# Turning the rotary halves: a float32 product on TensorE against a lane shuffle on VectorE

## The reference, cut to what matters

```python
def apply_partial_rope(x, cos, sin):
    half = ROPE_DIM // 2                      # ROPE_DIM = 16 of the 64 features of a head
    xr = x[..., :ROPE_DIM].astype(jnp.float32)
    x1, x2 = xr[..., :half], xr[..., half:]
    rot = jnp.concatenate([x1 * c - x2 * s, x2 * c + x1 * s], axis=-1)
    return jnp.concatenate([rot.astype(x.dtype), x[..., ROPE_DIM:]], axis=-1)

u = rmsnorm(x, norm_mix[l])
proj = u @ w_in[l]                            # q, k, v, iq, ik, iw, cB, cC, ch, g
q, k, iq, ik = (apply_partial_rope(...) for each)
y_attn = dsa_attention(q, k, v, iq, ik, iw) @ w_attn_out[l]
```

## Time and profile before

| | us |
|---|---|
| median of three runs | 1742.22 (1742.13 to 1742.66) |
| the profiled execution, device time | 1742.58 |
| its span in the trace | 1741.2 |
| TensorE busy with products | 1719.8 |
| VectorE busy | 1330.1 |
| ScalarE busy | 917.9 |

### The profile page before, as it was taken

How to read it: one execution, slowest core, us unless ns; L and a number is a source line. 1 busy time by engine, 2 the same in 40 slices (tenths; PEclk the granted TensorE clock), 3 DMA queues, 4 the chain that set the end, 5 groups by cost and what they waited for, 6 DMA issues and landing times.

```text
span 1741.2 us, 33420 instructions
## 1 busy us (share of the span) xinstructions
PE 1719.8 (99%) x11698; PEld 1582.1 (91%) x11698; DVE 1330.1 (76%) x2375; ACT 917.9 (53%) x1624; POOL 63.8 (4%) x113
## 2 busy tenths in 40 slices
PE   9999999999999999999999999999999999999997
PEld 8899899989999899999889999999999988888886
DVE  6986788778976788877765999988888766666666
ACT  4354544444454544455554555577777655555553
POOL 0000001000000122100000000000000000000000
PEclk9999999999999999999999999999999999999999
DMA  6556688754544699744344555554443456555654
GB/s 229 170 177 205 212 293 276 245 182 158 169 158 159 228 326 323 240 153 134 121 170 136 172 175 181 181 171 137 142 134 134 138 193 193 193 192 192 193 193 153
DMA packets 90250, 327.76 MB, mean 188 GB/s; under 512 B 11016, under 2 KB 11192, under 8 KB 89712
## 3 DMA queue, kind: packets, MB, share of 16 engines
q1 hardware_dynamic: 79056, 286.45, 49.6%
q0 software_dynamic: 9840, 34.82, 6.2%
q10 hardware_dynamic: 1264, 5.24, 0.8%
HBM read 324.34 MB, written 6.09 MB: 190 GB/s over the span
## 4 chain that ended last, share of the span: by engine, by line
PE 82%; DVE 13%; issue 2%; ACT 1%; DMA 1%; DVEq 0%; ACTq 0%; SPq 0%
PE bank L209 25%; PE bank L210 24%; PE bank L211 24%; DVE Z L86 6%; DVE w_lo L186 4%; PE bank L1767 3%; DVE yc L86 1%; PE bank L280 1%; PE bank L1325 1%; PE bank L480 1%; ACT w_hi L181 1%; DVE rows L86 0%; PE bank L773 0%; PE bank L1594 0%; PE bank L1181 0%
## 5 line engine op out<-in xcount | busy, mean ns | idle before, releaser
L186 DVE TENSOR_TENSOR w_lo<-raw,w_hi 128x1024 fp32r<-128x1024 f32 x544 | 658.8, 1221 | 157.1 <-ACT w_hi L181 156.0
L181 ACT ACTIVATE w_hi<-raw 128x1024 fp32r<-128x1024 f32 x544 | 572.3, 1054 | 260.6 <-PE bank L211 203.3
L209 PE MATMUL bank<-u_hi,w_hi 128*128 128x256 f32 x2400 | 692.9, 289 | 2.8 <-DVE Z L86 1.3
L210 PE MATMUL bank<-u_lo,w_hi 128*128 128x256 f32 x2400 | 678.7, 283 | 0.0
L211 PE MATMUL bank<-u_hi,w_lo 128*128 128x256 f32 x2400 | 678.6, 283 | 0.0
L209 PEld LDWEIGHTS bank<-u_hi,w_hi 128*128 128x128 f32 x2400 | 459.5, 191 | 15.5 <-issue 7.9
L210 PEld LDWEIGHTS bank<-u_lo,w_hi 128*128 128x128 f32 x2400 | 459.9, 192 | 4.4 <-issue 2.2
L211 PEld LDWEIGHTS bank<-u_hi,w_lo 128*128 128x128 f32 x2400 | 459.5, 191 | 0.0
L209 PE MATMUL bank<-w_hi,a_hi 128*128 128x512 f32 x744 | 290.3, 390 | 0.7 <-DVE u_lo L1853 0.7
L210 PE MATMUL bank<-w_lo,a_hi 128*128 128x512 f32 x744 | 290.1, 390 | 0.0
L211 PE MATMUL bank<-w_hi,a_lo 128*128 128x512 f32 x744 | 289.4, 389 | 0.0
(11 more groups left out here) (283 smaller groups left out, 1715.6 us busy)
## 6 DMA issues: line engine op xcount, KB each, us to landing
raw<-stream SPq DMA_DIRECT2D x544, 512.0 KB, 4.2
gate<-w_ada POOLq DMA_DIRECT2D x48, 512.0 KB, 6.0
t_rows<-t_by_distance POOLq DMA_DIRECT2D x8, 256.0 KB, 3.7
rpb_rows<-rpb_pad POOLq DMA_DIRECT2D x8, 224.0 KB, 4.2
bias_b<-rpb_rows POOLq DMA_DIRECT2D x16, 96.0 KB, 6.5
bias_a<-t_rows POOLq DMA_DIRECT2D x1, 1536.0 KB, 12.6
x<-x_in ACTq DMA_DIRECT2D x2, 512.0 KB, 5.7
gains_b<-gains POOLq DMA_DIRECT2D x1, 1024.0 KB, 9.3
```

The lines of the kernel that those rows point to most:

```text
L181: nc.scalar.activation(w_hi[:, s, :], raw[:, s, :], ACT.Copy).then_inc(s_hi, 1)
L186: nc.vector.tensor_tensor(w_lo[:, s, :], raw[:, s, :], w_hi[:, s, :].bitcast(F32), ALU.subtract).then_inc(s_split, 1)
L209: M.matmul(o, lh, rh, start=start, stop=False, skip_group_check=True)
L210: M.matmul(o, lh, rl, start=False, stop=False, skip_group_check=True)
```

## The change

The permutation is no longer a product. `rope` calls VectorE's `stream_shuffle`, which reorders partitions within each group of 32 by one list, `SWAP` (the first 8 lanes trade places with the next 8; where a group holds no rotary features the sine is 0, so that the order there does not matter). The sine product then reads the shuffled copy `rot` in SBUF instead of a bank. `ik` is turned on 64 partitions, and a second shuffle with the identity list copies it to the other 64.

`R` is no longer multiplied in when `k` and `ik` leave their banks: ScalarE copies them out as they are, and two new tables `RC` and `RS` (cosine and sine times `R`) made by VectorE right after `R` take its place. The table in DRAM is smaller (cosine and sine once each, no permutation matrices) and comes by one DMA instead of two.

```diff
+SWAP = [(p + ROPE // 2) % ROPE if p < ROPE else p for p in range(32)]
@@ main_part
                     if name == "ik":
-                        got["iwT"] = AC.go((m,), S.activation, ikT[DH:DH + 32, :], bank[b][DH:DH + 32, 0:T], ACT.Copy)
-                        ik_m = m
-                    elif name == "k":
-                        if f == 0:
-                            ik_m = VE.go((ik_m, got["R"], got["iwT"]), V.tensor_tensor, ikT[0:DH, :], bank[4][0:DH, 0:T],
-                                         R[0:DH, :], ALU.mult)
-                            got["ik", 0], free[4] = ik_m, (ik_m,)
-                        m = VE.go((m, got["R"]), V.tensor_tensor, d.rearrange("p (a n) -> p a n", a=parts),
-                                  bank[b][:, 0:parts * T].rearrange("p (a n) -> p a n", a=parts),
-                                  R.unsqueeze(1).to_broadcast([P, parts, T]), ALU.mult)
+                        m = AC.go((m,), S.activation, ikT[0:DH + 32, :], bank[b][0:DH + 32, 0:T], ACT.Copy)
                     else:
-                        m = AC.go((m,), S.activation, d, bank[b][:, 0:parts * T], ACT.Copy)
+                        m = AC.go((m,), S.activation, dst[:, f:f + 2, :].rearrange("p a n -> p (a n)"), bank[b][:, :],
+                                  ACT.Copy)
@@ the turn
-                t = PE.done(M.matmul(bank[b][:, 0:n], turn[:, 0:P], d, start=True, stop=True))
-                m = VE.go((t, got.get(("rot", b))), V.tensor_tensor, r, bank[b][:, 0:n],
-                          rope[:, 1, 0:n], ALU.mult)
-                m1 = VE.go((t, got[name, f]), V.tensor_tensor, d, d, rope[:, 0, 0:n], ALU.mult)
+                m = VE.go((got[name], got.get(("rot", slot))), V.stream_shuffle, r, d, SWAP)
+                m1 = VE.go((m,), V.tensor_tensor, d, d, cos, ALU.mult)
+                m = VE.go((m,), V.tensor_tensor, r, r, sin, ALU.mult)
                 m = VE.go((m, m1), V.tensor_tensor, d, d, r, ALU.add)
@@ rope_of_ik
-                for j in range(2):
-                    i = M.matmul(bank[b][:, j * T:(j + 1) * T], turn[0:DH, (1 + j) * P:(2 + j) * P], ikT[0:DH, :],
-                                 start=True, stop=True, skip_group_check=True)
+                m = rope(ikT[0:DH, :], rot[0:DH, 0, 0:T], (0, ("ik", 0)), RC[0:DH, :], RS[0:DH, :])
+                got["ik", 0, "r"] = VE.go((m, got["iw"]), V.stream_shuffle, ikT[DH:2 * DH, :], ikT[0:DH, :],
+                                          list(range(32)))
@@ side_part
                 m = VE.go((t,), V.tensor_copy, R, bank[6][:, 0:T])
+                VE.go((m,), V.tensor_tensor, RC, R, rope_t[:, 0, :], ALU.mult)
+                VE.go((m,), V.tensor_tensor, RS, R, rope_t[:, 1, :], ALU.mult)
                 got["R"] = VE.go((m,), V.tensor_tensor, R2, R, R, ALU.mult)
```

More of the change, by code:

```diff
@@ L516, in build @@
         ph1a = ph1.enter_context(ExitStack())
-        rope = sb(ph1a, "rope", [P, 2, 2 * T])
-        turn = sb(ph1a, "turn", [P, 3 * P])
+        rope_t = sb(ph1a, "rope", [P, 2, T])
+        rc_rs = sb(ph1a, "rc_rs", [P, 4, T])
+        RC, RS = rc_rs[:, 0, :], rc_rs[:, 1, :]
         cw_all = sb(ph1a, "cw_all", [P, LAYERS, KW * TAPS])
@@ L783, in rope_of_ik, with rope @@
-            def rope_of_ik():
[L785 to L788, removed]
-                for j in range(2):
-                    i = M.matmul(bank[b][:, j * T:(j + 1) * T], turn[0:DH, (1 + j) * P:(2 + j) * P], ikT[0:DH, :],
-                                 start=True, stop=True, skip_group_check=True)
[L792 to L799, removed]
+            def rope(d, r, names, cos, sin):
+                slot, name = names
+                VE.wait((s_rope, 16), got.get("R"))
+                m = VE.go((got[name], got.get(("rot", slot))), V.stream_shuffle, r, d, SWAP)
+                m1 = VE.go((m,), V.tensor_tensor, d, d, cos, ALU.mult)
+                m = VE.go((m,), V.tensor_tensor, r, r, sin, ALU.mult)
+                m = VE.go((m, m1), V.tensor_tensor, d, d, r, ALU.add)
+                got["rot", slot] = m
+                got[(*name, "r")] = m
+                return m
@@ new lines, in rope_of @@
+            def rope_of(name, dst, f, slot):
+                cos, sin = (a.unsqueeze(1).to_broadcast([P, 2, T]) for a in (
+                    (RC, RS) if name == "k" else (rope_t[:, 0, 0:T], rope_t[:, 1, 0:T])))
+                rope(dst[:, f:f + 2, :], rot[:, slot, :].rearrange("p (a n) -> p a n", a=2), (slot, (name, f)), cos, sin)
+            def rope_of_ik():
+                m = rope(ikT[0:DH, :], rot[0:DH, 0, 0:T], (0, ("ik", 0)), RC[0:DH, :], RS[0:DH, :])
+                got["ik", 0, "r"] = VE.go((m, got["iw"]), V.stream_shuffle, ikT[DH:2 * DH, :], ikT[0:DH, :],
+                                          list(range(32)))
@@ L820, in side_part @@
                 m = VE.go((t,), V.tensor_copy, R, bank[6][:, 0:T])
+                VE.wait((s_rope, 16))
+                VE.go((m,), V.tensor_tensor, RC, R, rope_t[:, 0, :], ALU.mult)
+                VE.go((m,), V.tensor_tensor, RS, R, rope_t[:, 1, :], ALU.mult)
                 got["R"] = VE.go((m,), V.tensor_tensor, R2, R, R, ALU.mult)
@@ L824, in side_part @@
                 take(6)
-                PE.wait(got["iwT"])
+                PE.wait(got["ik", 0])
                 for tt in range(NT):
@@ L1999, in rope_table @@
     cos, sin = np.ones((P, T), np.float32), np.zeros((P, T), np.float32)
-    turn = np.zeros((P, P), np.float32)
     for f in range(P):
@@ L2005, in rope_table @@
             sin[f] = np.sin(ang[:, d % half]) * (-1.0 if d < half else 1.0)
[L2006 to L2010, removed]
+    return np.concatenate([cos, sin], 1)
 def t5_table_of_distance():
```

29 lines of the change are left out of this document (8 added, 21 removed).

## The result

The changed kernel takes **1750.43 us** (median of 6 runs, 1749.53 to 1752.22) against 1742.45 for the kernel before on the same chip (6 runs, 1742.13 to 1742.88). The ratio is 1.0047, with a 95% interval of 1.0035 to 1.0059: slower by 8.0 us. The profiled execution was the slowest of the six, at 1752.22 us with a span of 1750.9, so it shows 9.7 us of span more than the one before, where the median shows 8.0.

What follows compares the result with a forecast made beforehand. Both engines were taken as full in this stage, with VectorE's turns deciding when attention starts: 1742.58 + 2.9 + 2.2 (lateness per layer) + 3.0 (slow clock) = 1750.7, stated as 1750.3 us against the median; range 1743.5 to 1755.

Steps and rivals of the forecast that it cites:

- Where the end is set: At the first attention product (line 425 before, 426 after): net VectorE work beyond its 0.6 and 0.3 us lead delays it.
- The large turn: One 512-column turn on VectorE: 1.99 us before, 2.85 after, so 0.86 more, shuffle priced as a tensor_tensor plus 0.08 load.
- The cheap shuffle: Rival: a large turn costs 0.35 us less, giving 1743, with up to 3 more for the clock; chance 14%.
- the dear one: Rival: the shuffle takes twice the time per element, 6.4 us more, 1756.7; chance 7%.
- Ahead of the first index scores: VectorE work up to the index scores: +0.04 us in the first layer, 0.9 earlier in the second.
- From there to line 426: Four turns add 3.44 us to VectorE; the first attention product comes 2.9 and 2.2 us later in the two layers.
- The stands: TensorE waits some 6 us per layer ahead of the attention scores, and 2 and 1 us for ikT.
- The slow clock: Lower TensorE clock after each 6 us stand: 1.5 us each, 3.0 in all, with ends of 0 and 6.
- The nearest rival, late without a slow clock: VectorE is late as forecast but TensorE's resting costs nothing: 1747.3 us; chance 24%.

Runs made afterwards that it cites:

- e5: Changed kernel with the attention issued two pieces later and two side-part steps taken out further on, so both parts end together; 1735.16 us.
- e3: Changed kernel with each shuffle of k and q made twice; 1757.03 us.
- e6: Changed kernel with k and q turned by float32 products on TensorE again, iq and ik keeping the shuffle; 1740.53 us.
- e9: Balanced kernel (attention two pieces later, two steps out) with index scores one piece later too and one step of second-tile exponentials taken out; 1738.51 us.
- e1: Changed kernel with 24 unneeded products of 512 columns put on TensorE ahead of the attention scores; 1746.18 us.
- e10: Balanced kernel (attention two pieces later, two steps out) with 7 unneeded products where TensorE stands for ikT in the first layer; 1734.89 us.
- e4: Changed kernel with the attention issued two pieces later, by two empty side-part steps ahead of it; 1742.27 us.
- e2: Changed kernel without the shuffles of k and q, which are then not rotated as the reference does; 1745.68 us.

## Why the prediction was right

The forecast was 1750.3 us and the time is 1750.4. The mechanism held; that the sum fits to 0.1 us is luck, since its terms do not.

- **Where the end is set.** Right. TensorE's spared products are real (e5 has 9.6 us less busy time with the dip in it, where I counted 10.3), and none of it reached the end, since line 426 waits for VectorE. The row that carried this was the earlier trace rows, one wait of 0.2 us in 46, against the 76% of the earlier trace rows. e3 doubles the shuffles and pays for each in full, e6 takes them away and the loss goes.
- **The large turn.** 2.71 us against 2.85. The tensor_tensor as the nearest row was the right choice: the shuffle takes 0.72 to 0.74 us, 0.77 from start to start. My error is the load of the lane list, which I priced at 0.08 after the earlier trace rows and which costs nothing. The cheap shuffle and the dear one both fall. What the Trainium skill, "VectorE: DVE Perf Modes", perf-mode tier table, says of the shuffle (one element per cycle only) agrees with this 0.74: with the 0.43 of the shuffle of 256 columns that is 1.2 ns per further column, and 2400 ns for 2048 is 1.2 too. The 0.6 that I had scaled from it was short by 0.14.
- **Ahead of the first index scores.** I said +0.04 for the first layer, and the scores start 0.60 earlier. Of that 0.43 is the earlier beginning of the execution, so that -0.17 stands against the +0.04: the turn of `iq` is 0.14 less than priced and that of `ik` 0.19 (2.21 for 2.40), and waits between the other rows give back 0.12. In the second layer I said -0.9 and it is -1.2 (417.95 - 5.05 - 414.12).
- **From there to line 426.** Four turns add 4 x 0.72 = 2.9, not 3.44. The leads were also smaller than I took them: from the end of the last addition to line 426 the signal takes 0.26 us (84.54 to 84.80, and 464.94 to 465.20), and I had taken off under 0.1, so VectorE was ready 0.40 and 0.10 early, not 0.6 and 0.3. By this account 2.9 - 0.17 - 0.40 = 2.3 and 2.9 - 1.2 - 0.1 = 1.6 us would be VectorE's own; by place it holds TensorE up by 2.00 and 1.55, where I said 2.9 and 2.2. This term was too large by 1.5; the 0.3 in the first layer I did not trace. The 3.04 measured there looks like my 2.9 only because the clock's dip after the shorter stand adds 1.47.
- **The stands.** About 6 us predicted in each layer, 5.80 and 6.38 measured. For `ikT` 2 and 1 predicted, 1.84 and 0.55 measured.
- **The slow clock.** The mechanism is right and its size was off, the other way: 3.0 predicted, 6.3 in the profiled execution, and 8.0 - 3.55 = 4.4 in the median. The start of the program was the wrong measure for a stand in the middle: here the clock stays at half for some 4 and 6 us after the work resumes, and 2.0 and 2.8 us are lost, not 1.5 each. The row itself also varies, from 6.00 us (after) to 7.63 (e9), and the clock column does not show that start: in the trace of after it reads 1.00 from 2 to 4 us with 6 products recorded, and from 4 to 6 us with 11. And I let only the two long stands count, while one of 1.84 us can do it. The rule that I cited from the Trainium skill, "TensorE: Matmul & The Clock Gate", on HAM oscillation (a long enough gap lowers the clock), is thus shown in mid-program by these rows and by e1, with the reservation that for stands of about 2 us length alone does not decide, as the last section says.

So the mechanism, the place and the size of the stands held, and the time came out to 0.1 us because two terms were off by like amounts in opposite directions, 1.5 too much for VectorE and 1.4 too little for the clock. The nearest rival, late without a slow clock at 1747.3, is struck by the rows at 0.50 and by e1.

I had also taken the order of the side part as given. The changed kernel does not gain, as I said, but a gain was there to be had in another order, 7.1 us under the kernel before (5.3 under the same order without shuffles), behind two empty steps ahead of line 426 and two steps less behind it.

## What to carry to other kernels

Work moved to an engine that is idle on the average is paid in full if, in the stage where it lands, that engine never waits and another waits for it: read its waits in that stage and the lead at the next place where the two meet, not its share. If the lead is too short, issue the consumer later and shorten the woven part elsewhere by as many steps, since two more steps alone only moved the stand to the end of the stage. And count a stand of TensorE with the slow clock behind it, 2.0 and 2.8 us here, which needless products in its place take away.

## What was not expected

- A stand of TensorE of 1.8 to 1.9 us, with full work before it, is followed by a granted clock of 0.50 in some executions and by none below 1.00 in others: 3 of 7 traces, with the numbers under e10. Of e9's two stands of 1.8 us one was and one was not, and e4's two of 2.27 us at the end of the stage were not. One of 0.55 us in the second layer never was, the two of 3.2 and 3.7 us in e2 and all longer ones were. What decides between the executions no run here shows.
- Such a dip is paid by way of VectorE: TensorE's work is late by it, VectorE waits 1.3 or 1.4 us, and TensorE then waits for VectorE 34 us further on, 1.47 us longer (after against e1).
- The load of the shuffle's lane list costs nothing (0.01 to 0.02 us beside the shuffle's own start), and the shuffle is only 0.05 us longer than a tensor_tensor of its size.
